# Halves of 256 tokens at three residual updates of a hybrid layer stack in near-fp32 arithmetic

## The reference, cut to what matters

```python
h = h + rmsnorm(y @ w_out, g_post)                      # residual A (first block)
gate = sigmoid(h @ w_pg); e = p_l @ w_pp
h = h + rmsnorm(gate * e, g_ple)                        # residual B
for l in range(2):                                      # second and third block
    proj = rms_norm(x, pre_norm_g[l]) @ w_in[l]         # ... retention, attention, gated recurrence
    x = x + rms_norm(mixed @ w_out[l], post_norm_g[l])  # residual C (l = 0), the end (l = 1)
```

## Time and profile before

| | |
|---|---|
| time, median of 3 runs | 3036.71 us (3035.82 to 3039.58) |
| the profiled execution | 3036.43 us, of it 3034.6 us span |
| mean granted TensorE clock | 0.991 |
| PE busy | 2955.4 us (97% of the span), 17162 matmuls |
| weight loads busy | 2385.6 us (79%) |
| DVE, POOL, ACT busy | 1649.8 us (54%), 1315.0 us (43%), 1284.9 us (42%) |

### The profile page before, as it was taken

One profiled execution on the slowest core, in us unless ns is written; L12 is line 12 of the kernel. 1 busy time (PEld: TensorE's weight loads), 2 busy tenths in 40 slices (PEclk: granted clock), 3 DMA queues, 4 the chain that ended last, 5 costly groups with the idle time before them and its releaser, 6 DMA issues.

```text
span 3034.6 us, 48369 instructions
## 1 busy us (share of the span) xinstructions
PE 2955.4 (97%) x17162; PEld 2385.6 (79%) x17162; DVE 1649.8 (54%) x2349; ACT 1284.9 (42%) x2468; POOL 1315.0 (43%) x1002
## 2 busy tenths in 40 slices
PE   8999999999999999989999999999999999999997
PEld 6888888877777787767887878788778878787886
DVE  5367666655656315657565664561275656654412
ACT  6545444354556333443333333453343333344432
POOL 4444444443433343553444444344444444444444
PEclk9999999999999999999999999999999999999999
DMA  6223222222222323233222222232242222222322
GB/s 238 102 90 111 83 83 76 77 84 83 78 77 80 125 97 139 90 118 125 105 87 91 87 85 82 83 142 100 104 156 88 95 87 96 84 84 80 143 97 97
DMA packets 60880, 305.72 MB, mean 101 GB/s; under 512 B 5712, under 2 KB 6096, under 8 KB 29776
## 3 DMA queue, kind: packets, MB, share of 16 engines
q1 hardware_dynamic: 38224, 259.54, 24.0%
q10 hardware_dynamic: 22528, 44.50, 4.2%
HBM read 285.67 MB, written 18.35 MB: 100 GB/s over the span
## 4 chain that ended last, share of the span: by engine, by line
issue 56%; POOL 32%; PE 9%; POOLq 1%; DMA 1%; ACT 1%; DVE 0%; DVEq 0%; ACTq 0%; SPq 0%
POOL w_low L262 31%; PE z L325 8%; DMA w_raw<-in_wt 1%; POOLq L261 1%; POOL next_weights L270 0%; PE scores L325 0%; PE v_bank L358 0%; PE z L358 0%; ACT u_high L722 0%; DVE mixed L1647 0%; POOLq L296 0%; DVE work L1266 0%; POOLq L284 0%; POOLq L129 0%; ACT w_high L710 0%
## 5 line engine op out<-in xcount | busy, mean ns | idle before, releaser
L262 POOL TENSOR_TENSOR w_low<-w_raw,w_high 128x512 fp32r<-128x512 f32 x932 | 1254.3, 1350 | 1700.0 <-ACT w_high L710 1692.5
L325 PE MATMUL z<-u_high,w_high 128*128 128x512 f32 x3408 | 1347.6, 395 | 2.6 <-POOL w_low L262 1.8
L325 PE MATMUL z<-u_high,w_low 128*128 128x512 f32 x3408 | 1328.4, 390 | 0.0
L325 PE MATMUL z<-u_low,w_high 128*128 128x512 f32 x3408 | 1327.0, 389 | 0.0
L710 ACT ACTIVATE w_high<-w_raw 128x512 fp32r<-128x512 f32 x928 | 578.7, 628 | 1223.0 <-PE z L325 1128.3
L325 PEld LDWEIGHTS z<-u_high,w_high 128*128 128x128 f32 x3408 | 640.1, 188 | 160.2 <-issue 23.3
L325 PEld LDWEIGHTS z<-u_high,w_low 128*128 128x128 f32 x3408 | 639.6, 188 | 136.1
L325 PEld LDWEIGHTS z<-u_low,w_high 128*128 128x128 f32 x3408 | 640.5, 188 | 127.1
L1633 DVE TENSOR_TENSOR work<-work 128x512 f32<-128x512 f32 x87 | 99.9, 1148 | 365.0 <-ACT work L947 351.7
L1260 DVE TENSOR_TENSOR work<-z,work 128x512 f32<-128x512 f32 x110 | 76.1, 692 | 122.7 <-PE z L325 101.8
L1292 DVE SCALAR_TENSOR_TENSOR work<-z,work 32x512 f32<-32x512 f32 (+1 forms) x176 | 120.9, 687 | 2.4
(11 more groups left out here) (281 smaller groups left out, 3243.7 us busy)
## 6 DMA issues: line engine op xcount, KB each, us to landing
w_raw<-in_wt SPq DMA_DIRECT2D x241, 1024.0 KB, 4.8
out_hT<-work ACTq DMA_DIRECT2D x8, 1024.0 KB, 8.7
work<-out_hT ACTq DMA_DIRECT2D x8, 1024.0 KB, 10.4
work<-in_xT SPq DMA_DIRECT2D x4, 1024.0 KB, 17.2
e_scratch<-work ACTq DMA_DIRECT2D x1, 4096.0 KB, 16.7
work<-in_xT ACTq DMA_DIRECT2D x4, 1024.0 KB, 10.9
work<-in_dec ACTq DMA_DIRECT2D x12, 256.0 KB, 2.7
work<-rope_tables ACTq DMA_DIRECT2D x10, 256.0 KB, 2.8
```

What stands on the lines that cost most here:

```text
L262: pool.tensor_tensor(WL[:, 4 * q:4 * q + 4, :], RAW[:, t.odd, 512 * q:512 * q + 512].rearrange("p (k c) -> p k c", k=4), WH[:, 4 * q:4 * q ...
L325: mm = pe.matmul(bank[:], w[:, k, :], u[:, k, :], start=(k == 0 and n == 0), stop=(k == KT - 1 and n == 2))
```

## The change

At the three seams the tokens are cut in two halves of 256. The last output tile runs as 48 matmuls on the first half and then 48 on the second (`split_tile`), so that the first half's squares, sum, root and residual can be done while PE is at the second half. `three_tiles` runs all 16 `k` for the first half, then all 16 for the second, with every matmul at 256 columns and the weights loaded in both halves. The second half's eviction, sum and root stand inside the first half of the opening three tiles on every engine. ACT now rounds the first opening weight tile before it evicts tile 14, and the second behind the first half's square. DVE goes through the 16 tiles twice, at 256 tokens each time. The last residual of the kernel is as it was.

```diff
+        SPLIT_BANK, SUM_BANK, ROOTS = [TP[0], VB], SC[1], [TP[1], SC[1]]
+        HALVES = [slice(0, S // 2), slice(S // 2, S)]
...
+            def three_tiles(t, gen, g, n, at):
+                pe.wait_ge(sem("z_free"), t.times(1, -T_HGG - 1))
+                for half, cols in enumerate(HALVES):
+                    for q in range(4):
+                        if half == 0:
+                            pe.wait_ge(sem("l_ready"), t.times(4, 8 + q + 1))
+                        for k in range(4 * q, 4 * q + 4):
+                            if half == 0:
+                                pe.wait_ge(sem("u_half"), g * 16 + k + 1)
+                            else:
+                                pe.wait_ge(sem("u_ready"), gen * 16 + k + 1)
...
+                            for x, bank in enumerate((Z[0], Z[1], SC[0])):
+                                for i, (w, u) in enumerate(((hi, UH), (hi, UL), (lo, UH))):
+                                    mm = pe.matmul(bank[:, cols], w[x], u[:, k, cols], start=(k == 0 and i == 0),
+                                                   stop=(k == KT - 1 and i == 2))
+                            if half == 0 and k == at:
+                                sum_second_half(n)
+                        if half == 1:
+                            mm.then_inc(sem("w_free"), 3)
+            def split_tile(t, n, g, at):
...
+                            for i, (w, u) in enumerate(((WH, UH), (WH, UL), (WL, UH))):
+                                mm = pe.matmul(SPLIT_BANK[half][:, cols], w[:, k, :], u[:, k, cols], start=(k == 0 and i == 0),
+                                               stop=(k == KT - 1 and i == 2))
+                        if half == 1:
+                            mm.then_inc(sem("w_free"), 1)
+                            if q == at:
+                                sum_first_half(n, g)
+                    if half == 0:
+                        mm.then_inc(sem("z_half"), 1)
...
+            split_tile(Tile(T_OUT + 15), 16, 0, 0)
+            three_tiles(Tile(T_PG), 2, 0, 16, 1)
...
+            split_tile(Tile(T_PG + 15), 32, 1, 2)
...
-                three_tiles(Tile(T_L2 + l * PER_LAYER), l * 2 + 3)
+                three_tiles(Tile(T_L2 + l * PER_LAYER), l * 2 + 3, l + 1, 64 if l else 32, 1 if l else 4)
...
+            def operand(t, g, new, second, scale=None, done=None):          # ACT
+                n = t.times(4)
+                steps = {0: lambda: high(t.plus(1), 1, n - 2), 3: lambda: high(t.plus(1), 2, n - 1), 5: lambda: high(t.plus(1), 3, n)}
+                for half, cols in enumerate(HALVES):
+                    for m in range(KT):
...
+                        act.activation(UH[:, m, cols], W[:, H + m, cols], ACT.Copy,
+                                       scale=1.0 if scale is None else scale[:, m:m + 1]).then_inc(sem("uh_ready" if half else "uh_half"), 1)
+                        if half == 0 and m in steps:
+                            steps[m]()
+                        if half == 0 and m in second:
+                            second[m]()
+                        if half and m in (7, 11, 13, 15):
...
+                            if q < 3:
+                                high(t.plus(2), q, n + 3 + 3 * q)
...
+                    act.activation(row(SQ1)[:, a], SPLIT_BANK[0][:, a], ACT.Square).then_inc(sem("sq_half"), 1)
+                    copy(MIX[:, 15, a], SPLIT_BANK[0][:, a], scale=gain[:, 15:16])
+                    for q in range(4):
+                        high_apart(t.plus(17), q, 1)
+                        if q == 1:
+                            root_half(0, (sem("sum_half"), split + 1), "root_half")
                     high(t.plus(17), 0, t.times(4, 61))
...
+            pg_slot(Tile(T_PG + 14), 14, 0, ((13, 1, 14),), ahead=Tile(T_L2))
             pg_square(14, 0, 15)
+            act.wait_ge(sem("sq_used"), PRIMED + 32 + 14)
+            pg_evict_half(0, (sem("z_half"), 2), "ze_half")
             for q in range(4):
                 high_apart(Tile(T_L2 + 1), q, 1)
+            pg_square_half(0, (sem("pg_half"), 1), "sq_half")
+            root_half(0, (sem("sum_half"), 2), "root_half")
+            high(Tile(T_L2 + 1), 0, 4 * T_L2 - 3)
...
+                for half, cols in enumerate(HALVES):                         # DVE, new_operand
...
+                    for m, k in ((0, 1), (1, 1), (2, 2), (4, 2), (6, 2), (8, 2), (10, 2), (12, 2), (14, 2)):
...
+                        v.tensor_tensor(MIX[:, m:m + k, cols], MIX[:, m:m + k, cols], b, ALU.mult)
+                        v.drain()
+                        x = W[:, H + m:H + m + k, cols]
+                        v.tensor_tensor(x, x, MIX[:, m:m + k, cols], ALU.add).then_inc(sem("h_new" if half else "h_half"), k)
+                        while lows < m:
+                            low_half(lows, n, g, half, scale)
+                            lows += 1
+                        if half == 0 and m in between:
+                            between[m]()
...
+            pg_last_half(0, (sem("ze_half"), 1), "pg_half")
...
+                new_operand(l + 2, l * 32 + 48, l + 1, l * 64 + 64, PR2[:, l, G2_PRE:G2_PRE + 16],
+                            {} if l else {2: lambda: pg_last_half(1, (sem("z_free"), T_PG + 16 - T_HGG), "pg_prod")})
```

More of the change, by code:

```diff
@@ L648, in _ @@
                         quarter(Tile(T_OUT + s, (2, i)), q)
-            sum_rows_last(16)
-            three_tiles(Tile(T_PG), 2)
+            for q in range(4):
+                quarter(Tile(T_OUT + 14), q)
+            split_tile(Tile(T_OUT + 15), 16, 0, 0)
+            three_tiles(Tile(T_PG), 2, 0, 16, 1)
             for m in range(3, 6):
@@ L900, in step @@
                         gate_sigmoid(gates + s)
[L902 to L927, removed]
@@ L935, in squares, with out_slots, one @@
                         high(t, m // 4)
-            def out_slots(t, n, gain, root, loads=(), last="next", pair=False):
-                def one(tt, m, s, used, first=False, quarters=4, taken=None, bank=None):
+            def out_slots(t, n, gain, root, loads=(), last="next", pair=False, split=None):
+                def one(tt, m, s, used, first=False, quarters=4, taken=None, bank=None, ahead=None):
                     for q in range(quarters):
@@ L943, in one @@
                             high(tt, q)
+                    if ahead is not None:
+                        ahead()
                     act.wait_ge(sem("w_free"), tt.times(4, 4) if taken is None else taken)
@@ L1118, in pg_square, with pg_slot @@
                 copy(MIX[:, m, :], MIX[:, m, :], scale=PR1[:, G_PLE:G_PLE + 16][:, bass.ds(m, 1)])
[L1120 removed]
+            def pg_slot(t, m, s, squares, bank=None, ahead=None):
                 for q in range(4):
@@ L1124, in pg_slot @@
                         pg_square(*squares[q // 2])
+                if ahead is not None:
+                    for q in range(4):
+                        high_apart(ahead, q, 0)
                 pg_evict(t, s, m + 31, bank)
@@ L1135, in _, with pg_evict_half, pg_square_half @@
                     pg_slot(Tile(T_PG + s, (2, i)), m, s, ((i * 2 + (s - 1), 1 - s, i * 2 + s),))
-            pg_slot(Tile(T_PG + 14), 14, 0, ((13, 1, 14),))
-            for q in range(4):
-                high_apart(Tile(T_L2), q, 0)
+            def pg_evict_half(half, wait, done):
+                c = HALVES[half]
+                act.wait_ge(*wait)
+                act.activation(row(SQ1)[:, c], SPLIT_BANK[half][:, c], ACT.Exp, scale=-1.0).then_inc(sem(done), 1)
+            def pg_square_half(half, wait, done):
+                c = HALVES[half]
+                act.wait_ge(*wait)
+                act.activation(row(SQ1)[:, c], MIX[:, 15, c], ACT.Square).then_inc(sem(done), 1)
+                act.drain()
+                copy(MIX[:, 15, c], MIX[:, 15, c], scale=PR1[:, G_PLE + 15:G_PLE + 16])
@@ L1237, in _ @@
                           loads=(lambda: act.wait_ge(sem("h_stored"), l * 64 + 64), behind_second),
-                          last="three" if l + 1 < LAYERS else "none", pair=True)
+                          last="three" if l + 1 < LAYERS else "none", pair=True, split=l + 2)
             n = LAYERS * 16 + 16
```

155 lines of the change are left out of this document (104 added, 51 removed).

## The result

The changed kernel takes 3046.08 us (median of 11 runs, 3043.92 to 3048.37) against 3036.61 us (11 runs, 3035.7 to 3039.58): a ratio of 1.0031, 95% interval 1.0023 to 1.0038. That is 9.5 us slower, beyond the 6 us that a measurement here can tell from no change, and 1.1 us above the top of the forecast's range. The forecast was 3036.5, no change.

What follows compares the result with a forecast made beforehand. PE, busy 97% of the span, plus its pauses bounds the kernel; the change can touch 44 us. Terms -1.3 + 0.6 - 0.4 + 1.0 = -0.1 us on 3036.43, with the median 0.3 above, gave 3036.5 us, range 3030 to 3045.

Steps and rivals of the forecast that it cites:

- Most of it is absorbed ... about 0.5 us is left. At B and C that is 1.0 us.: Behind the opening, state stores and squares start 2.7 us later against PE; only 0.5 us each at B and C remains.
- the walk at B: Going through the engines' lists at seam B: PE's opening starts at 8.7 and ends at 51.6, 0.6 us later than before.
- the standstill within tile 15: At seam B PE, inside tile 15's second half, stands from -0.4 to 3.1, 3.5 us.
- rival 3: Clock falls in the new standstills: A 0.7 us later, B 0.4 to 2.0, C 0.5; 3038 to 3040 us; chance 0.25.
- the spacing of 0.120 us: PE's 256-column matmuls follow each other every 0.120 us, making the opening's 288 take 34.6 us instead of 32.7.
- rival 1: PE's weight load does not hide at 256 columns: 3044 us at 0.14 us spacing, 3093 at 0.19; chance 0.11.
- the starts at A and C: PE's opening matmuls at seams A and C start at 4.5 and 4.4 us from the seam's zero; A's was 7.7.
- the 0.9 us for each of POOL's parts: In the opening, each POOL operation that excludes DVE costs DVE about 0.9 us, some 7 us at each seam.
- Rival 2: DVE and POOL hinder each other less at half size: 3021 us with no exclusions, 3029 with half; chance 0.13.
- Rival 4: Some wait put at nothing (loads of `e`, longer instruction lists) costs over 2 us a seam: 3043 or more; chance 0.06.
- the 1.3 us for the spacing by the formula: With the Trainium skill's 109 ns spacing at 256 columns, the three seams would be about 1.3 us shorter in all.
- the 0.8 us of a walk: Accuracy claimed for tracing the engines' lists through a seam: the old lists' computed ends match measured ones to 0.8 us.

## Why the prediction was wrong

**The step that failed: "Most of it is absorbed ... about 0.5 us is left. At B and C that is 1.0 us."** Its first half was right: the copies end 3.2 us before the opening does (forecast 3.3), and the squares start 2.5 us later against PE. But little or nothing of it is absorbed. From the first square to the sum there are 20.7 us before and 21.4 now at B (1397.54 to 1418.22, 1403.08 to 1424.49), and in front of a PE that was already waiting there is no slack. The 2.5 and the 0.7 are the 3.2 us that the wait grew by; the clock adds 1.5. Behind C the squares start 2.4 us later against PE, the chain takes 20.0 us instead of 20.6 (2226.94 to 2247.51, 2237.41 to 2257.37), and the wait grows by 1.7; with halves at B alone B does the same. So what the chain absorbs is 0.6 to 0.7 us where I had counted on about 2. I had put 1.0 for what was 8.2 in the profile, 6.0 by the medians. The quarter that waits for the end of the opening (1.11 us at 1401.20) and the next one (1.04 us at 1403.92) wait no more, at 1405.53 the first runs in its turn; these waits were the reserve, and they gave back only a part of their length. Why the chain is 1.4 us longer at B when the seams ahead are halved too is open: the extra time is idle time of DVE between its adds (5.2 against 3.7 us), in which it waits for nothing that the profile shows.

**The second: the walk at B, 51.6, was 55.4.** The start of the opening (9.7, forecast 8.7) and the standstill within tile 15 (3.5, as forecast) were near; the one before `k` = 2 was 1.96 us for 3.4, behind matmuls that took longer. What the walk left out is that the second root stands in ACT's list in front of nine copies and waits for PE. ACT stood there for 4.72 us. An estimate from the spacings gives 2.5 of them to the clock (26 matmuls at 0.216 instead of 0.120); the other 2.2 would have been there without it. The whole supply stood. I had priced the clock's fall (rival 3) at 0.4 to 2.0 us, as if only PE slowed down. Moving the root gave 3.9 us with the sum moved and 2.8 without, and the walk's 51.6 was then 51.7 and 52.8.

**Right:** the spacing of 0.120 us, so rival 1 (the load does not hide) is out; the starts at A and C (4.2 and 4.4, forecast 4.5 and 4.4); C's end (45.7, forecast 45.3); the first scale of DVE at A at -1.5 (forecast -1.6). Less near: the same at B, 5.8 for 4.6; the wait of PE at L377 at B, 0.5 for 1.3. **DVE and POOL:** the 0.9 us for each of POOL's parts was right for the lows (1.91 for two that take 0.88) and too much for the adds of 256 columns (0.98 to 1.03 for one of 0.43, so 0.6). Rival 2 is out all the same, although it would have been the way to a faster kernel: taking the three parts out of DVE's way in the second half gave 7.2 us, 6.4 of them in the second halves of its profile. (The Trainium skill, GPSIMD Engine Reference, Specifications, has the interfaces of POOL shared with VectorE operations of two inputs; the trace agrees, POOL's part taking 1.26 us alone and 1.75 beside DVE.) Rival 4, a wait put at nothing, is what happened with the root at B, a place that it didn't name; the wait behind the seams was in the sum, at 1.0.

Two slips of the prediction change nothing: its sum gives 3036.6, not 3036.5, and the 1.3 us for the spacing by the formula has no working (384 half matmuls a seam at 0.011 us less would be 4.2 us of PE's time at each; 1.3 in all takes the supply for the bound).

That A won 2.7 instead of 1.3 in the profile is more than the 0.8 us of a walk, and it is luck: in this execution alone the clock did not fall at A. With halves at A alone it fell, and the profile has 1.4, the medians 2.1. Not settled is how much of the loss at B is the clock by itself: no run here kept the clock up through B's standstills. Where it was up for a part, ACT's wait in the root was 1.15 us shorter and the seam 0.7 us (halves at B alone).

## What to carry to other kernels

When a supply is brought nearer to its consumer, follow what is queued behind the supplier: a chain of nearly fixed length (here 20 to 21.4 us of squares and adds) that began in the supplier's spare time now starts later against the consumer, and if the consumer waits at its end already, most of it counts. An instruction that waits for a slow engine belongs behind the work that this engine needs next; a root at `k` = 6 that nobody needs before the end of the pass cost 3 to 4 us, and not at the wait itself but later, where the lost lead no longer covered other pauses. One profiled execution can have the clock on its side, as here at A; compare a stretch over several before its gain is believed. And before splitting work finer, try the cheap moves on the kernel as it is: two of them gave 4.9 us without any halves.

## What the runs showed of the hardware

A weight load of 0.19 us (187 to 192 ns) hides behind matmuls of 256 columns that follow each other every 0.120 us. At B PE's clock fell behind a standstill of 3.5 us (0.53 over 1353.2 to 1355.7), was at 0.50 from 1357 to 1370, with pauses in between, and was back at 1.00 by 1371 in a stream; with halves at B alone it was up and down in turn over the same stretch. At A the clock stayed at 1.00 behind a standstill of 2.60 us in the changed kernel (the first nine matmuls 0.12 us apart), and was at 0.50 behind one of 2.65 with the sum later (over 1164.9 to 1168.2). The 1.75 us that POOL's part takes beside DVE is 0.5 more than alone, and the two lows of DVE beside it take 1.0 more. A reciprocal of 256 elements took 1.75 us where 512 take 3.35.
